# Hybrid encoder step on one core: the order of the query tiles in the forgetting attention, and the masked blocks of its bias

## The reference, cut to what matters

```python
def _fox_attend(q, k, v, cq, ck, qpos, kpos):
    scale = FOX_HEAD_DIM ** -0.5
    s = jnp.einsum('bqhd,bkhd->bhqk', q.astype(jnp.float32), k.astype(jnp.float32)) * scale
    s = s + jnp.transpose(cq, (0, 2, 1))[:, :, :, None] - jnp.transpose(ck, (0, 2, 1))[:, None, :]
    s = jnp.where(kpos[None, :] <= qpos[:, None], s, -jnp.inf)
    p = jax.nn.softmax(s, axis=-1)
    o = jnp.einsum('bhqk,bkhd->bqhd', p, v.astype(jnp.float32))
    return o.astype(q.dtype)

def _fox_prompt(q, k, v, logf):
    c = jnp.cumsum(logf, axis=1)
    # blocks of Q_BLOCK = 128 queries against all keys
```

## Time and profile before

| | |
|---|---|
| runs | 2004.11, 2004.02, 2005.10 us; median 2004.11 |
| profiled execution | 2003.76 us |
| its span in the profile | 2002.0 us (1.8 us lie around it) |
| mean granted clock of PE | 0.995 |
| PE busy | 1952.9 us (98 %), 11667 matmuls |
| DVE, ACT, POOL busy | 986.6, 631.5, 196.8 us (49, 32, 10 %) |
| chain that ended last, by engine | PE 85 %, DVE 4 %, issue 4 %, ACT 3 %, DMA 2 %, POOL 2 % |

### The profile page before, as it was taken

The page is one execution under the profiler, slowest core; times in us unless marked ns, Lnnn a source line. Parts: engine busy times, 40 slices in busy tenths (PEclk is TensorE's granted clock), DMA queues, the critical chain, the costliest instruction groups (busy, mean ns, idle before and its releaser), DMA issues.

```text
span 2002.0 us, 28721 instructions
## 1 busy us (share of the span) xinstructions
PE 1952.9 (98%) x11667; PEld 1921.4 (96%) x11667; DVE 986.6 (49%) x1886; ACT 631.5 (32%) x1198; POOL 196.8 (10%) x280
## 2 busy tenths in 40 slices
PE   7998999999989999999999999999999999999998
PEld 7998999999989999999999999999999999999998
DVE  6674545454546565563434464444444444444434
ACT  6444435353535444442223332111111111111112
POOL 0003424150601122000000000000000000000000
PEclk9999999999999999999999999999999999999999
DMA  6442221313165633453323311020202020111202
GB/s 182 117 108 61 80 64 43 100 34 94 50 214 180 192 99 121 139 164 106 97 82 86 90 42 38 27 58 27 58 27 58 27 58 27 55 30 54 74 22 95
DMA packets 208088, 164.24 MB, mean 82 GB/s; under 512 B 15310, under 2 KB 186318, under 8 KB 207445
## 3 DMA queue, kind: packets, MB, share of 16 engines
q1 hardware_dynamic: 207957, 162.41, 26.8%
HBM read 132.86 MB, written 29.51 MB: 81 GB/s over the span
## 4 chain that ended last, share of the span: by engine, by line
PE 85%; DVE 4%; issue 4%; ACT 3%; DMA 2%; POOL 2%; SPq 0%; POOLq 0%; ACTq 0%; DVEq 0%
PE ps L1239 71%; PE ps L1223 3%; PE ps L1075 2%; PE ps L1063 2%; PE ps L996 1%; PE ps L1006 1%; PE ps L1030 1%; POOL fox_p L860 1%; PE ps L911 1%; PE ps L1145 1%; PE ps L983 1%; DMA foxs_kraw<-in_cache_fox_k_dram 0%; DVE prod L2086 0%; ACT fox_pt_hi L1396 0%; ACT w_hi L443 0%
## 5 line engine op out<-in xcount | busy, mean ns | idle before, releaser
L1239 PE MATMUL ps<-act_hi,w_hi 128*128 128x384 f32 x1800 | 612.9, 341 | 5.4 <-DVE fox_v L2071 4.0
L1239 PE MATMUL ps<-act_hi,w_lo 128*128 128x384 f32 x1800 | 604.0, 336 | 0.0
L1239 PE MATMUL ps<-act_lo,w_hi 128*128 128x384 f32 x1800 | 603.6, 335 | 0.0
L1239 PEld LDWEIGHTS ps<-act_hi,w_hi 128*128 128x128 f32 x1800 | 339.3, 188 | 7.2 <-issue 6.4
L1239 PEld LDWEIGHTS ps<-act_lo,w_hi 128*128 128x128 f32 x1800 | 339.5, 189 | 0.7
L1239 PEld LDWEIGHTS ps<-act_hi,w_lo 128*128 128x128 f32 x1800 | 339.0, 188 | 0.0
L443 ACT ACTIVATE w_hi<-w_raw 128x512 fp32r<-128x512 f32 (+1 forms) x172 | 147.2, 856 | 302.3 <-PE ps L1239 300.7
L461 DVE TENSOR_TENSOR w_lo<-w_raw,w_hi 128x512 fp32r<-128x512 f32 (+1 forms) x172 | 168.1, 978 | 131.8 <-ACT w_hi L443 131.8
L1239 PE MATMUL ps<-ff_hi,w_hi 128*128 128x384 f32 x672 | 227.0, 338 | 0.0
L1239 PE MATMUL ps<-ff_lo,w_hi 128*128 128x384 f32 x672 | 227.0, 338 | 0.0
L1239 PE MATMUL ps<-ff_hi,w_lo 128*128 128x384 f32 x672 | 227.0, 338 | 0.0
(11 more groups left out here) (308 smaller groups left out, 2824.7 us busy)
## 6 DMA issues: line engine op xcount, KB each, us to landing
w_raw<-in_w_in_dram SPq DMA_DIRECT2D x44, 512.0 KB, 4.4
w_raw<-in_w_up_dram SPq DMA_DIRECT2D x32, 512.0 KB, 4.1
w_raw<-in_w_down_dram SPq DMA_DIRECT2D x56, 256.0 KB, 2.7
merged<-prod SPq DMA_DIRECT2D x48, 192.0 KB, 1.9
prev<-merged SPq DMA_DIRECT2D x48, 192.0 KB, 4.3
foxs_kraw<-in_cache_fox_k_dram SPq DMA_DIRECT2D x8, 1024.0 KB, 5.5
foxs_vraw<-in_cache_fox_v_dram SPq DMA_DIRECT2D x8, 1024.0 KB, 5.7
out_dram<-fin_y SPq DMA_DIRECT2D x9, 512.0 KB, 2.7
```

The lines of the kernel that those rows point to most:

```text
L1239: last = nc.tensor.matmul(bank(b)[:, 0:width], W[k][a][:, t, :], moving[z][:, t, j * width:(j + 1) * width], start=(t == 0 and n == 0), st ...
```

## The change

Both heads take their tiles from the last to the first. A masked block is then never seen again in its head, so `keep` and the two store tiles go, nothing is put back, and POOL has one mask per unit: `MASKS` is 16 per pair instead of 31, and DVE waits for s + 1 of them. The mask of unit s waits until unit s - 1 has been read, except for the first unit of each head.

```diff
-        kept = [tensor(f"negc_kept{k}", [P, P], C_AT + 512 + 512 * k) for k in range(2)]
...
         def query_tile(u):
-            return u % QT if u // QT % 2 == 0 else QT - 1 - u % QT
+            return QT - 1 - u % QT
...
-        MASKS = 4 * QT - 1
+        MASKS = 2 * QT
 
         def masked_by(s):
-            return (2 if s == 0 else min(3 * s + 3, 3 * QT)) if s < QT else 2 * QT + s
+            return s + 1
...
-            def keep(i):
-                next_mask(nc.gpsimd.tensor_copy(kept[i % 2][:], own(0, i)))
-                mask(0, i)
-
             def bias(p, s):
                 if s == 0:
                     pool.wait_ge(at_s["negc_in"], 16 * (p + 1))
-                    keep(0)
-                    keep(1)
-                    mask(1, QT - 1)
-                elif s != QT:
+                elif s % QT:
                     pool.wait_ge(at_s["s_read"], 16 * p + s)
-                    if s < QT:
-                        next_mask(nc.gpsimd.tensor_copy(own(0, s - 1), kept[(s - 1) % 2][:]))
-                        if s + 1 < QT:
-                            keep(s + 1)
-                    else:
-                        mask(1, 2 * QT - 1 - s)
+                mask(s // QT, query_tile(s))
```

## The result

The changed kernel takes 2020.32 us (median of 4 runs, 2015.67 to 2021.62), the kernel before 2004.61 in the same series: a ratio of 1.0076, 95 % interval 1.0064 to 1.0088. It is slower by 15.7 us; the forecast was 2018.0 us, slower by 14.3. The profiled execution took 2021.62 us, its span is 2019.9 us, 17.9 above the 2002.0 of before.

A forecast was written before the change was run, and what follows sets the result against it. PE was taken as the bound, so only stops of its queue count: 3 pairs at +4.2 us (+3.1 and +1.1) plus 1.7 for pair 0 gives +14.3 on 2003.76, 2018.1 us (predicted 2018.0); 8-in-10 range 2010 to 2027.

The forecast's parts named there:

- PE as the bound, POOL's own work at 0 us: PE is busy 98 % of the span; POOL's 15 dropped operations per pair lie in idle time, 0 us by themselves.
- The start of a pair, +3.1 us: First head: bank -0.81, scores of unit 1 +0.62, of unit 2 +0.75, turns of unit 0 +1.40, unit 1 +1.14.
- The second head, +1.1 us: Per pair, new waits of 0.6 us in slot 10 and 1.5 at unit 9's turn, less 1.0 of old stops.
- The 1.0 us of old stops: Second head: the 0.42 and 0.32 us waits and two short stops at units of 8, 8, 7 blocks would go.
- The reason for the turns of units 1 and 9: Mask behind POOL's division, then read, exp and halves come late; PE waits 1.14 us (unit 1) and 1.5 (unit 9).
- Pair 0, +1.7 us: First pair: slow products at the lower clock cover two waits; 0.6 us at unit 1's turn plus 1.1 in the second head.
- The clock rival: New stops at a pair's start bring PE's lower clock: 9 us more, 2027 us; chance 0.10.
- No change: Rival: PE's work is unchanged and two slots' slack takes up the longer steps, 2003.8 us; chance 0.06.
- faster: Rival: POOL's shorter queue lets reads run early and saves today's PE stops, 7.4 us, 1996.4 us; chance 0.07.

The follow-up runs named there:

- masks' run with unit 8's mask first: Kernel before (old order) with POOL's masks only, no copies or putting back, unit 8's mask made at the pair's start: 2002.40 us, ratio 0.9985 to 1.0004.
- the run with copies: Changed kernel with POOL's 15 dropped operations per pair put back as copies into the store tile: 2020.29 us, ratio 1.0066 to 1.0100.
- the mirror: Changed kernel with the second head ascending (8 to 1, then 1 to 8 blocks), needed putting back left out: 2013.81 us, ratio 1.0036 to 1.0066.
- run of the first three edits: Changed kernel with ACT splitting weights before unit 0's exp, 8-block divisions on DVE, and pair 0's bias loaded earlier: 2005.42 us, ratio 1.0002 to 1.0021.
- the run with the swap in ACT's queue: Changed kernel; in slots 2 and 10 ACT copies the turned 8-block unit's high halves before the newest unit's exp: 2005.32 us, ratio 0.9998 to 1.0016.
- the four edits: On the changed kernel: weights' split before exp, 8-block divisions on DVE, ACT's halves before exp, pair 0's bias loaded earlier; all together 1991.18 us.
- the same with early bias: Changed kernel with pair 0's bias loaded at the start of kturn instead of vturn: 2014.84 us, ratio 1.0040 to 1.0073.
- the split ahead: Changed kernel, but in a pair's first slot ACT splits the next weights before unit 0's exp: 2012.37 us, ratio 1.0032 to 1.0062.
- DVE's division: Changed kernel with the 8-block units (0 and 8) divided by DVE instead of POOL: 2013.26 us, ratio 1.0036 to 1.0066.
- the old order with early bias and halves first: Kernel before, pair 0's bias loaded at kturn, ACT's halves before the exp in slots 8 and 10: 1993.94 us, ratio 0.9939 to 0.9964.

## Why the prediction was right, and where it was not

**PE as the bound, POOL's own work at 0 us: right.** The masks' run with unit 8's mask first says so, and the run with copies for 14 of 15 operations. A small cost of the mask part was missed: the mask of unit 8 stood at the pair's start, and when it comes in unit order it can stand behind a division. In the old order that is 0.5 us per pair; in the new one the division ahead of it is of 2 blocks, and DVE's read of unit 8 does not wait.

**The start of a pair, +3.1 us.** Measured, in the forecast's order: -0.76 at the bank (forecast -0.81), +0.44 (0.62), +0.44 (0.75), +1.02 (1.40), +0.90 (1.14): +2.04. All five are there, in order and place; the rows of the four stops are each 0.2 to 0.4 us below the forecast's terms. Much of that is how a stop is counted. A row counts from the modelled end of the matmul before it, 0.34 us after its start, while in a running queue the next one starts after 0.173 us. So the scores of unit 1, at 292.32 behind a product that started at 291.54, are 0.61 us later than a running queue would have them, for 0.62 forecast, and the row says 0.44. The busy time agrees: per pair it is 104.30 us in the old order with one stop left, 104.66 in the kernel before, and 105.33 in the changed kernel with seven stops, for the same matmuls.

**The second head, +1.1 us.** 0.20 and 1.80 us measured for 0.6 and 1.5. The 1.0 us of old stops that the forecast takes off was too much: of PE's idle time some 0.5 us went, the 0.32 and 0.2 of short ones. The 0.42 us that it counts in full were a wait of the weight loads, behind which the scores of unit 8 started only 0.28 us late (309.28, after a product at 308.83). The sum of PE's idle time per pair, 5.29 less 1.75, is 3.54 us: 2.04 at the start, 1.5 in the second head. With the 0.67 us of busy time this is the period's difference of 4.21; 4.2 was forecast. The places and the size of the whole are right; that the sum meets to 0.01 us is luck, since its two halves are off in opposite directions.

**The reason for the turns of units 1 and 9: half wrong.** The prediction lists mask, read, exp and then the halves, and puts the start of that row down to the mask that stands behind POOL's division. The mask does make DVE wait (1.04 us for unit 2's, 0.24 for unit 10's), but with the division off POOL the stops stayed at 1.09 and 1.87. What decided was the step behind it: halves that are ready at PE stand in ACT's queue behind an exp that is not. With these swapped neither stop is left, although POOL divides and masks as in the changed kernel.

**Pair 0, +1.7 us: mis-sized.** It was 4.05 us. Its second head had the stop of 1.80, and behind it PE's granted clock fell to the lower level; here is the changed kernel from 220 us on:

```profile
220.00:222.00 2.00, 0.85 (x6) 0.61 (x4) 0.73 (x1) 1.59 (x3) 0.42 (x2) 1.00 0.28 85
222.00:224.00 2.00, 1.36 (x8) 1.39 (x9) 1.64 (x6) 0.00 (x0) 0.94 (x1) 0.72 0.00 0
224.00:226.00 2.00, 2.00 (x8) 2.00 (x8) 0.84 (x1) 1.73 (x3) 1.51 (x2) 0.50 0.00 0
226.00:228.00 2.00, 2.00 (x13) 1.91 (x12) 0.51 (x4) 0.00 (x0) 1.51 (x1) 0.93 0.00 0
```

The granted clock lacks 0.28, 0.50 and 0.07 in three stretches of 2 us, which is 1.7 us of work. With 4.05 - 1.7 the rest is 2.35 us, against 1.7 forecast; the mirror and the run with copies, whose records show no such episode there, have 2.5 and 2.8 us.

**The clock rival** had been placed at the pair's start, at 0.10. It came, but at the restart, in one pair of four, and for half as long as in pair 0's beginning. The run of the first three edits shows it in two pairs, each time behind the stop of 1.83; this is pair 2:

```profile
428.00:430.00 2.00, 0.19 (x2) 0.22 (x3) 1.56 (x4) 0.79 (x2) 0.00 (x0) 1.00 0.09 24
430.00:432.00 2.00, 2.00 (x12) 2.00 (x11) 1.06 (x5) 1.20 (x2) 1.77 (x1) 0.71 0.00 0
432.00:434.00 2.00, 2.00 (x8) 2.00 (x8) 0.91 (x2) 0.53 (x2) 1.60 (x3) 0.50 0.00 0
```

That pair takes 109.71 us instead of 108.18. A stop of 1.8 us can thus cost 3.3 (1.8 and the pair's 1.53). In the run with the swap in ACT's queue there was neither the stop nor the lower clock behind it. It is also the likely reason why medians moved by more than the sum of the pairs; that was read from one execution per run and not shown for the timed ones.

**No change and faster** are out. The Trainium skill ("Perfetto Trace Analysis", "Identifying the Most-Contended Engine") has TensorE's headroom judged by the busy share of its weight loads. Read strictly, with these at 95 % and the work unchanged, that gives +0, and the measurement is +15.7 us. The Trainium skill's section "Optimization Strategy", in "Perfetto Trace Analysis" too, tells to look for the gaps on that engine and for what blocks them. That fits this case: each of the four edits began at a listed stop of PE.

The sum came out close, 14.3 against 15.7 us, and not all of that is merit: in the period the terms of the start that were too large and the second head's that was too small cancel, and the clock that was left out (1.7 us in the profiled execution) is about what is missing.

## What to carry to other kernels

Where one engine is busy all the time and the others stand in a ring behind it, reordering the units changes no work and can still cost time (here 15.7 us of 2004): before it, go through the first two or three large units queue by queue. In each in-order queue look for an instruction that is ready behind one that waits; here ACT's exp before its copy was worth 15.0 of the 15.7 us that the change had lost. And take away the long stop first: the bias load of the first pair alone gave more (7.7 us) than any order of the units.

## What the runs showed of the hardware that was not expected

A stop of 1.8 us on PE was followed by the lower clock in some pairs only: 1 of 4 in the changed kernel, 1 of 4 in the same with early bias, 2 of 4 in the run of the first three edits, and none of 4 each in the runs with copies, with the split ahead and with DVE's division, at stops of 1.77 to 1.87 us throughout. That is 4 of 24. The same place in the program meets it or not. Whether this sets the scatter of a kernel's runs is not shown: the four runs of the changed kernel lie within 6 us and those of the kernel with copies, with the same stop, within 1.7; five runs of the old order with early bias and halves first, without it, within 5.8.

DVE multiplies a 128 x 1024 float32 tile by a column in 0.75 us, and POOL in 2.85; DVE's read with bias and row extreme of the same size takes 1.22 us.
